# Block products for w_ff1, and longer blocks for w_ff2, in a two-layer float32 trunk on one core

## The reference

```python
for l in range(DEPTH):
    cond = c_act @ w_ada[l] + b_ada[l]
    sh_a, sc_a, ga_a, sh_m, sc_m, ga_m = [v[:, None, :] for v in jnp.split(cond, 6, axis=-1)]
    ...
    h = rmsnorm(x, g_mlp[l]) * (1.0 + sc_m) + sh_m
    x = x + ga_m * (jnp.square(jax.nn.relu(h @ w_ff1[l])) @ w_ff2[l])
return rmsnorm(x, g_final)
```

## Time and profile before

| | us |
|---|---|
| median of 3 runs | 3222.48 (3220.72 to 3223.18) |
| span of the profiled execution | 3222.4 |
| PE busy | 3126.9 (97%) |
| DVE busy | 1979.7 (61%) |
| ACT busy | 1098.5 (34%) |
| POOL busy | 1676.9 (52%) |
| DMA | 280.99 MB, 87 GB/s |

### The profile page before, as it was taken

How to read it: one execution, slowest core, us unless ns; L and a number is a source line. 1 busy time by engine, 2 the same in 40 slices (tenths; PEclk the granted TensorE clock), 3 DMA queues, 4 the chain that set the end, 5 groups by cost and what they waited for, 6 DMA issues and landing times.

```text
span 3222.4 us, 40885 instructions
## 1 busy us (share of the span) xinstructions
PE 3126.9 (97%) x15021; PEld 2549.3 (79%) x15045; DVE 1979.7 (61%) x2633; ACT 1098.5 (34%) x1993; POOL 1676.9 (52%) x1781
## 2 busy tenths in 40 slices
PE   8999999998999999999999999999989999999998
PEld 6878887776788888888878888867668888888887
DVE  7872256887665666655578532578765655555555
ACT  2124314766222222222220342356651222222233
POOL 3557632233463555666745585222334566666665
PEclk8999999999999999999999999999999999999999
DMA  7444541001522222211234457200115221111112
GB/s 263 143 157 131 160 117 27 1 1 33 177 85 80 79 79 79 72 47 53 79 131 138 144 155 187 66 1 1 34 34 176 72 80 53 53 53 49 50 46 105
DMA packets 301358, 280.99 MB, mean 87 GB/s; under 512 B 11115, under 2 KB 275559, under 8 KB 300648
## 3 DMA queue, kind: packets, MB, share of 16 engines
q1 hardware_dynamic: 282002, 212.90, 22.7%
q10 hardware_dynamic: 19158, 65.47, 5.4%
HBM read 232.20 MB, written 38.80 MB: 84 GB/s over the span
## 4 chain that ended last, share of the span: by engine, by line
PE 85%; DVE 10%; issue 2%; ACT 2%; POOL 1%; DMA 0%; ACTq 0%; DVEq 0%; POOLq 0%
PE lin L1451 45%; PE lin L1881 16%; PE lin L1598 8%; PE aux L1740 2%; DVE pTL L2643 2%; DVE negm L2619 2%; PE pv L1756 2%; PE pv L1757 1%; PE lin L1716 1%; PE lin L1787 1%; PE lin L1717 1%; PE pv L1556 1%; ACT pTH L2203 1%; PE lin L1682 1%; PE lin L1501 1%
## 5 line engine op out<-in xcount | busy, mean ns | idle before, releaser
L1291 POOL TENSOR_SCALAR unit<-wraw 128x512 fp32r<-128x512 f32 x340 | 289.9, 853 | 775.0 <-PE lin L1451 272.4
L1451 PE MATMUL lin<-hH,unit 128*128 128x512 f32 x1824 | 577.2, 392 | 0.5 <-POOL wlo L1293 0.5
L1451 PE MATMUL lin<-hL,unit 128*128 128x512 f32 x1824 | 572.8, 390 | 0.0
L1451 PE MATMUL lin<-hH,wlo 128*128 128x512 f32 x1824 | 572.4, 389 | 0.0
L1293 POOL TENSOR_TENSOR wlo<-wraw,unit 128x512 fp32r<-128x512 f32 x340 | 489.1, 1438 | 28.4
L1881 PE MATMUL lin<-fH,unit 128*128 128x512 f32 x1568 | 486.9, 390 | 5.3 <-DVE xT L2778 5.3
L2778 DVE SCALAR_TENSOR_TENSOR xT<-lin,adac,xT 128x512 f32<-128x512 f32 x448 | 328.9, 749 | 183.1 <-PE lin L1881 178.4
L1451 PEld LDWEIGHTS lin<-hH,wlo 128*128 128x128 f32 x1824 | 342.4, 188 | 72.1
L1451 PEld LDWEIGHTS lin<-hL,unit 128*128 128x128 f32 x1824 | 342.4, 188 | 71.8 <-issue 0.2
L1451 PEld LDWEIGHTS lin<-hH,unit 128*128 128x128 f32 x1824 | 339.2, 188 | 70.4 <-issue 2.3
L1881 PEld LDWEIGHTS lin<-fH,unit 128*128 128x128 f32 x1568 | 294.3, 188 | 68.3 <-POOL unit L1326 3.9
(11 more groups left out here) (353 smaller groups left out, 5719.3 us busy)
## 6 DMA issues: line engine op xcount, KB each, us to landing
wraw<-in_w_ff SPq DMA_DIRECT2D x136, 512.0 KB, 4.0
wraw<-in_w_ada SPq DMA_DIRECT2D x80, 512.0 KB, 3.8
wraw<-in_w_in SPq DMA_DIRECT2D x72, 512.0 KB, 4.9
mix_keep<-tmp ACTq DMA_DIRECT2D x32, 512.0 KB, 6.2
wraw<-in_w_o SPq DMA_DIRECT2D x24, 512.0 KB, 4.2
adar<-in_w_ada SPq DMA_DIRECT2D x16, 512.0 KB, 11.8
x_keep<-xT ACTq DMA_DIRECT2D x4, 2048.0 KB, 9.3
gate_keep<-ropes ACTq DMA_DIRECT2D x16, 512.0 KB, 3.6
```

What stands on the lines that cost most here:

```text
L1291: pool.tensor_scalar(high, raw, 1.0, 1.0, ALU.mult, ALU.mult).then_inc(w_hi, 1)
L1451: mm = pe.matmul(lin[c % 2][:, hf], w, m(k, hf), start=first, stop=last)
```

## The change

- 28 of the 32 w_ff1 tiles of a layer are done in 14 pairs by seven block products of 4 row blocks, all in one run behind f1 3. The data's forms of h are made by DVE behind the norm (`hg_piece`, `hg_low`), in place where h's own parts lie.
- The result of a hidden pair comes out by half banks: ACT copies four, DVE adds four, squares four and makes the four sums (t1 to t4) for w_ff2; ACT stores all eight blocks, 2 MB a pair, in HBM (hid_keep). f1 0 to 3 are squared by ACT and stored too (hid_first).
- w_ff2 then runs in three blocks of eight row tiles, 12 pairs by products of 12 matmuls, whose data forms come back from HBM on SP's queue, 1 MB each, each behind the product that used its place; ACT makes the high part and DVE the low part, 2048 columns wide. One late group of four row tiles keeps products of 6 matmuls, and f1 0 to 3 stay dense.
- xT's rows 2 to 7 are put away (x_keep) and come back before the output pairs; in between they hold the copies, the sums and two w_ada tiles.
- w_ada tiles are issued two a pair behind the hidden pairs 3 to 12, and multiplied in pairs 2 to 11. POOL makes the sums of a following pair between the low parts of the one at hand, across w_ff1 and w_ff2.

```diff
+CLASSIC = FG
+BLOCK = 2 * FG
+BLOCKS = (D_FF // P - CLASSIC) // BLOCK
+HID_PAIRS = (D_FF // P - CLASSIC) // 2
+ADA_HID = range(2, 2 + (N_ADA - ADA_GATE) + ADA_FIRST - sum(ADA_WO) // 2)
...
+        for p in range(HID_PAIRS):
+            for kind, f in zip(("mate", "wide"), hidden_tiles(p)):
+                tiles.append((kind, layer, "w_ff1", 0, P * f, KC, ("hid", p)))
...
+        for q in range(FULL_BLOCKS):
+            for j, kind in enumerate(("mate", "wide")):
+                tiles.append((kind, layer, "w_ff2", P * (CLASSIC + BLOCK * (q // QUADS)), P * (2 * (q % QUADS) + j), KC, ("out", q)))
...
+            def load_forms(sp, g, before, lo, hi):
...
+                for i in range(lo, hi):
+                    sp.wait_ge(prod_done, PRODUCTS * KIND_NO[before] + (i if g < BLOCKS else i // 2) + 1)
+                    sp.dma_start(moving_full[i][:, :, :] if g < BLOCKS else late(moving_full, i), kept_block(g, i)).then_inc(hid_in[i], 16)
...
+                def hidden_products(p):
...
+                    for i in range(PRODUCTS):
+                        if p == 0 and i in HG_READY:
+                            pe.wait_ge(hg_lo, 8 * layer + HG_READY[i])
+                        pe.wait_ge(form_lo, PRODUCTS * KIND_NO[n] + i + 1)
...
+                        seven(n, i, moving, home[bank_turn(p)[ROLE[WIDE_ROLE_ORDER[i]]]])
...
+                        if q % QUADS == 0:
+                            pe.wait_ge(hid_lo, HID_LAYER * layer + PRODUCTS * (q // QUADS) + i + 1)
...
+                def quadrant(p, which):
...
+                    dve.tensor_tensor(c, home[bank_turn(p)[role]], c, ALU.add).then_inc(g_add, 1)
...
+                for q in range(FULL_BLOCKS):
+                    g, last = q // QUADS, q % QUADS == QUADS - 1
...
+                    for m in range(EVICTED):
+                        evict(HID_PAIRS + q, m, (WIDE_EVICTIONS, WIDE_AFTER))
+                        if last and m in (3, 4, 5, 7):
+                            hid_low(g + 1, (3, 4, 5, 7).index(m))
+                        if q % QUADS == 0 and m < 3:
+                            hid_low(g, 4 + m)
```

888 lines of the change are left out of this document (537 added, 351 removed).

## The result

The changed kernel takes 3239.8 us (median of four runs, 3235.8 to 3241.2) and the kernel before, on the same chip, 3221.6 (3219.4 to 3223.2): a ratio of 1.0054, 95% interval 1.004 to 1.0068. It is slower by 17 us where 14 less were forecast. The profiled execution has a span of 3234.0 us.

A forecast was written before the change was run, and what follows sets the result against it. PE, busy 97% of 3222.4 us and paying for every matmul, was taken as the bound; 3222.4 - 76.2 removed + 62 of new holes (18 + 4 + 20 + 14 + 6) = 3208 us, range 3166 to 3246.

The forecast's parts named there:

- Place 1: Into the first block product, once a layer: DVE's 28 operations and POOL's turns make it late, 9 us a layer.
- Place 2: Hidden pairs with w_ada: DVE needs 20.5 us of 19.1 in ten pairs, ten us free; 4 us, layer 0 only.
- Place 3: Last hidden pair to first output block, once a layer: PE waits for DVE's 2048-wide low parts, 10 us a layer.
- Place 4: Block to block, twice a layer: seven low parts and eight evictions exceed PE's 19.1 us; 3.5 us each.
- late group: The late group of w_ff2, with half-size forms: the same hole as from block to block, 3 us a layer.
- What is removed: w_ff1 pairs fall from 96 to 84 matmuls, 21.77 to 19.08 us; with w_ff2 76.2 us in all.
- the root: Hidden pairs without w_ada: PE's pitch is 19.1 us, with POOL's 16.3 of 19.1 given no price.
- The turn: DVE operations reading two SBUF tensors and POOL operations slow each other: up to 1.2 us of DVE's time per meeting.
- case 3: w_ada pairs: each of POOL's 11 operations takes a whole turn from DVE, 24.9 us a pair; 3252 us, chance 0.14.
- The stores: Hidden pairs' stores, 2 MB a pair in 19 us, lie beside PE and cost nothing.
- case 4: Form loads at output blocks: at 4.65 us a MB products start 6 us later, six times; 3246 us, chance 0.08.
- The clock: In the new holes: no falls to the lower level counted, left to the range; 1.5 us was named for one.

The follow-up runs named there:

- e1: Changed kernel with only the last of each w_ada tile's four products made beside the hidden pairs (part left out): 3219.2 us, ratio 0.9992.
- e2: Changed kernel with four places instead of two for w_ada tiles, whole computation: 3242.6 us, ratio 1.0066.
- e6: Changed kernel with the three full blocks' low parts made for one of four k tiles only (part left out): 3201.3 us, ratio 0.9939.
- e5: Changed kernel with ScalarE making the first output block's operand highs of forms 3 to 6 one form later: 3234.7 us, ratio 1.0041.
- e4: Changed kernel with a hidden pair's store from the sums' buffer issued before the one from the quadrants' buffer: 3233.4 us, ratio 1.0036.
- e14: Kernel with sums stored first, first low part earlier and w_ada spread (3214.9 us), with 8 instead of 20 VectorE subtractions per layer before the hidden pairs: 3205.2 us.
- e8: Changed kernel with 14 extra matmuls ahead of the first hidden and first output pair's first product in each layer: 3240.1 us, ratio 1.0055.
- e11: Kernel with sums stored first, first low part earlier and w_ada spread (3214.9 us), with seven filler matmuls at the second and third output blocks' turns: 3220.4 us.
- e16: Kernel with sums stored first, first low part earlier, w_ada spread and e5's order (3214.1 us), with another ScalarE order at the first block products: 3219.0 us.

## Why the forecast was wrong, by its steps

Holes in us, as the forecast put them and as the pitches show them (0.5 for w_ada's columns taken off):

| step | forecast | layer 0 | layer 1 |
|---|---|---|---|
| Place 1, into the first block product | 9 a layer | 11.5 | 11.5 |
| Place 2, pairs with w_ada | 4, layer 0 | 17 | 1 |
| Place 3, to the first output block | 10 a layer | 14.6 | 13.5 |
| Place 4, two turns | 7 a layer | 8.4 | 8.5 |
| late group | 3 a layer | 5.5 | 5.3 |
| holes that the kernel before had there | in the start value | -4 | -3 |
| in all | 62 | 53 | 37 |

- **What is removed** was right: 19.04 us a pair, 19.08 forecast, and the pairs of layer 1 without w_ada have it, though GpSimd is busy 134 of 152 us there. That was named as the root, and it holds.
- **The turn** was the right mechanism. The Trainium skill's "SBUF — State Buffer", Who interferes with whom, gives an exclusive lock for the whole instruction. The low parts' rows agree with it (2.29 and 1.29 alone, 3.3 to 3.4 on both engines in a row). The forecast took half a turn for w_ada against that rule, from one row of seven products in 7.20 us. That row stood beside a GpSimd with gaps. Beside the full one each product took 1.23 us on average, 1.4 in a row of four, and 1.51 when only one of four was left.
- **Place 2** is the step that failed, 4 forecast against 17 and 1. A pair costs VectorE 21.7 us (130.04 for six), not 20.5; in ten pairs that is 26 over 19.1 instead of 14. Of these 1.2 us a pair 1.1 is the term that was mis-sized, the eight w_ada products: between 1130 and 1301 us the 49 that add took 60.1 us and the seven that begin a tile 4.5, together 9.2 for each of seven pairs, where 8 times 1.01 was taken. (The 20.5 itself doesn't follow from its words. Nine turns of at most 0.9 us on 11.7 make 19.8, and the 512-wide row shows 0.4 for a turn, not 0.9. The 512-wide operations came out near it all the same, at 9.9 us a pair, which was luck.) The free lead was right at 8 to 10. This is case 3's mechanism at somewhat under half its price (24.9 a pair); it was given 0.14, and the sign the forecast named for it, a pitch over 19.5 from the sixth pair on, is there. e1 and e2 show it is VectorE and not the queue.
- **Place 3** had the right order and the right releasers but was too small by 4 a layer. Two things were priced at nothing: GpSimd's side of each turn, 2.0 us a meeting, which the chain of waits runs over from 1312 us on (how many of the 4 us are its is not shown, as e6 takes both sides away), and ScalarE behind a load (e5: 0.7 to 0.9 a layer by the pitches).
- **The stores** "lie beside PE and cost nothing" was wrong: 6.4 us, by e4. They were on VectorE's way through a buffer that is single. These microseconds lie in the rows of Places 2 and 3 and are not a further one.
- **Loads** (case 4) of 1 MB took a median of 7.3 us in the largest group, more than the 5.7 forecast. They showed up only through ScalarE's order; the turns' holes went in e6 with the loads as they were, and so did not belong to case 4.
- **Place 1** was 2.5 a layer too small (1.5 ahead of a plain tile, 3.3 ahead of the pair, 6.7 in it), and its chain was right (VectorE's 28 operations, e14). Place 4 was near too, and the late group, less the 2.7 us that the kernel before had in its own, is what was said.
- **The clock** was left out of the sum, and in these holes rightly: nine falls at the 1.5 us that the forecast named for one would have been 13. Fillers took five falls away in two kernels, and nothing came back (e8, e11). As a rule it would be wrong, by e14 and e16, which lost some 3 and 5 us to falls.
- **Range and chances.** 3239.8 lies in the stated range, but the kernel was to be faster and is slower. The range didn't reach case 3's own 3252, though it was said to take in nearly all of the slower cases; and case 4's six times 6 us make 3244, not 3246.

The sum's 62 stand against 90 by this table and 88 by the spans; half of the difference is Place 2. With 26 for 14 there the forecast would have said 3220, no change; the other half lies at Places 1, 3 and 4 and in the late group: 2.5 us a layer ahead of and in the first block product, and at the change, where GpSimd's side of the turns and the stores have a share.

## What to carry to other kernels

Price two engines that exclude each other from rows in which both are full, and price it on both: at the low parts VectorE paid 0.4 to 1.1 us for a meeting and GpSimd 2.0. Before work is moved into an engine's slack, look for the stretches in which that slack is already spoken for, and keep it out of those: the same sixteen tiles cost 17 us beside one set of pairs and next to nothing beside another. Where a wait moves from one engine to the other under each new order, look for less work on one of the two. And read a fall of the clock by what stands behind it: where TensorE runs into another engine's wait it is free, where TensorE runs on it is paid.
